# Orders of VectorE and ScalarE around seven waits of TensorE in a two-layer mixer and FFN kernel

## The reference, cut to what matters

```python
mod = (silu(c) @ ada_w[l] + ada_b[l])            # 6 vectors of 1024: shift, scale, gate, twice
h = rms_norm(x, mix_pre_g) * (1 + scale_m) + shift_m
q, k, v, x_lru, gate = split(h @ w_in)
attn = sliding_window_attention(rope(q), rope(k), v, sinks)      # window 128
lru  = rg_lru(causal_dwconv(x_lru)) * gelu(gate)                 # recurrence over the tokens
y = concat(rms_norm(attn), rms_norm(lru)) @ w_out
x = x + gate_m * rms_norm(y, mix_post_g)
h = rms_norm(x, ffn_pre_g) * (1 + scale_f) + shift_f
g, val = split(causal_dwconv(h @ w_up))                          # 2 x 3072
x = x + gate_f * rms_norm((gelu(g) * val) @ w_down, ffn_post_g)
```

## Time and profile before

| | |
|---|---|
| median of 3 runs | 1156.53 us |
| profiled execution, its own time | 1151.1 us |
| its span | 1149.3 us |
| TensorE (PE) busy | 1115.9 us, 97% |
| VectorE (DVE) busy | 803.3 us, 70% |
| ScalarE (ACT) busy | 569.6 us, 50% |
| `lo_chunk`, L1146 | 221.0 us, 182 of 1221 ns |
| `split_step`, L604 | 189.6 us, 182 of 1053 ns |
| mean granted clock of TensorE | 0.991 of full speed |

### The profile page before, as it was taken

One profiled execution on the slowest core, in us unless ns is written; L12 is line 12 of the kernel. 1 busy time (PEld: TensorE's weight loads), 2 busy tenths in 40 slices (PEclk: granted clock), 3 DMA queues, 4 the chain that ended last, 5 costly groups with the idle time before them and its releaser, 6 DMA issues.

```text
span 1149.3 us, 14253 instructions
## 1 busy us (share of the span) xinstructions
PE 1115.9 (97%) x5638; PEld 936.3 (81%) x5638; DVE 803.3 (70%) x1229; ACT 569.6 (50%) x958; POOL 52.1 (5%) x110
## 2 busy tenths in 40 slices
PE   6999899999999999999998999999999999999997
PEld 6986688888788888888888777898888888888886
DVE  7999987777678776777565797777643665356545
ACT  4488948544134422343377895765422444134431
POOL 3000110000210011000000000000000000000000
PEclk7999999999999999999999999999999999999999
DMA  9853373333765558643132421322232232233221
GB/s 357 337 205 110 100 285 111 128 112 127 270 242 202 167 191 290 158 150 125 55 111 74 93 74 59 102 98 92 96 106 92 92 103 81 91 114 107 92 92 74
DMA packets 49284, 159.88 MB, mean 139 GB/s; under 512 B 9409, under 2 KB 9665, under 8 KB 49217
## 3 DMA queue, kind: packets, MB, share of 16 engines
q1 hardware_dynamic: 33968, 118.57, 30.7%
q0 software_dynamic: 10368, 37.75, 9.9%
q10 hardware_dynamic: 4880, 2.64, 0.9%
HBM read 156.83 MB, written 2.11 MB: 138 GB/s over the span
## 4 chain that ended last, share of the span: by engine, by line
PE 77%; DVE 13%; ACT 5%; DMA 4%; issue 2%; SPq 0%; DVEq 0%; ACTq 0%
PE ps L1832 48%; PE ps L1857 27%; DVE sb_wL L1146 3%; DMA sb_raw<-in_w 1%; ACT sb_wH L604 1%; DMA sb_vw<-in_ada 1%; DMA sb_adaw<-in_ada 1%; DVE sb_x L1224 1%; DVE sb_stage L1152 1%; DVE sb_adaw L1152 1%; PE ps L1945 1%; DVE sb_y L1191 1%; ACT sb_sq L736 1%; DVE sb_xc L1452 1%; DVE sb_vw L1152 0%
## 5 line engine op out<-in xcount | busy, mean ns | idle before, releaser
L1832 PE MATMUL ps<-sb_hH,sb_wH 128*128 128x512 f32 x832 | 325.4, 391 | 0.5 <-ACT sb_xc L807 0.5
L1832 PE MATMUL ps<-sb_hL,sb_wH 128*128 128x512 f32 x832 | 323.8, 389 | 0.0
L1832 PE MATMUL ps<-sb_hH,sb_wL 128*128 128x512 f32 x832 | 323.8, 389 | 0.0
L1146 DVE TENSOR_TENSOR sb_wL<-sb_raw,sb_wH 128x1024 fp32r<-128x1024 f32 x182 | 221.0, 1221 | 78.7 <-ACT sb_wH L604 78.3
L604 ACT ACTIVATE sb_wH<-sb_raw 128x1024 fp32r<-128x1024 f32 x182 | 189.6, 1053 | 163.5 <-DMA sb_raw<-in_w 163.3
L1857 PE MATMUL ps<-sb_wH,sb_mH 128*128 128x512 f32 x512 | 202.2, 395 | 4.6 <-DVE sb_wL L1146 4.6
L1857 PE MATMUL ps<-sb_wL,sb_mH 128*128 128x512 f32 x512 | 199.4, 389 | 0.0
L1857 PE MATMUL ps<-sb_wH,sb_mL 128*128 128x512 f32 x512 | 199.4, 389 | 0.0
L1832 PEld LDWEIGHTS ps<-sb_hH,sb_wH 128*128 128x128 f32 x832 | 156.2, 188 | 37.6 <-issue 4.3
L1832 PEld LDWEIGHTS ps<-sb_hH,sb_wL 128*128 128x128 f32 x832 | 156.2, 188 | 32.5
L1832 PEld LDWEIGHTS ps<-sb_hL,sb_wH 128*128 128x128 f32 x832 | 156.2, 188 | 31.8
(11 more groups left out here) (222 smaller groups left out, 1136.5 us busy)
## 6 DMA issues: line engine op xcount, KB each, us to landing
sb_raw<-in_w SPq DMA_DIRECT2D x182, 512.0 KB, 3.5
sb_adaw<-in_ada POOLq DMA_DIRECT2D x42, 512.0 KB, 4.9
sb_stage<-in_ada SPq DMA_DIRECT2D x24, 512.0 KB, 14.2
sb_vw<-in_ada POOLq DMA_DIRECT2D x20, 512.0 KB, 4.9
sb_raw<-in_w SPq DMA_DIRECT2D x8, 384.0 KB, 14.3
sb_stage<-in_ada POOLq DMA_DIRECT2D x6, 512.0 KB, 4.2
sb_x<-in_x SPq DMA_DIRECT2D x4, 512.0 KB, 5.6
sb_x<-in_xt SPq DMA_DIRECT2D x4, 512.0 KB, 6.6
```

Of the source, the lines that this page charges most:

```text
L1146: TT(low_of(n), raw_of(n), high_of(n).bitcast(fp32), ALU.subtract).then_inc(w_lo, 1)
L1832: return nc.tensor.matmul(out, a, b, start=start, stop=stop, **kw)
```

## The change

The same instructions are issued as before; on ScalarE and VectorE some stand elsewhere. TensorE, SyncE and POOL keep their programs.

```diff
 # ScalarE, tile_chains, k = 1 (once: the end of the first layer)
                     y_square(l, k, 1, 2)
                     y_root(l, k, 2)
+                    split_step(n0 + 4)
                     x_root(l, k, 2)
                     x_scaled(l, k, 2)
+                    split_step(n0 + 5)
                     y_square(l, k, 1, 3)
                     y_root(l, k, 3)
+                    tmp_lower(l, k, 2)
...
                 x_root(l, k, 3)
                 x_scaled(l, k, 3)
-                if k:
-                    split_step(n0 + 4)
-                    split_step(n0 + 5)
-                tmp_lower(l, k, 2)
+                if not k:
+                    tmp_lower(l, k, 2)
 # ScalarE, mixer of the first layer
                     copy_pt(1)
                     gate_tanhs(1)
-                    decays(1)
                     square_out(1)
                     attn_high(1)
                     gate_tanhs(2)
+                    decays(1)
+                    gate_out(1)
                     split_step(O0 + 3)
                     decays(2)
-                    gate_out(1)
                     gate_out(2)
 # VectorE, tile_chains
                 x_update(l, k, 3)
-                x_recip(l, k, 3)
                 if k:
                     lo_chunk(n0 + 4)
+                x_recip(l, k, 3)
+                tmp_upper(l, k, 2)
+                if k:
                     lo_chunk(n0 + 5)
-                tmp_upper(l, k, 2)
 # VectorE, mixer of the first layer
                     mod_unit(25)
-                    drives(1)
+                    attn_low(1)
                     gated(1)
                     mod_unit(26)
-                    attn_low(1)
                     gated(2)
+                    drives(1)
...
                     drive(0)
+                    attn_low(2)
                     scan(0)
                     drive(1)
-                    attn_low(2)
...
                     product(1)
+                    lo_chunk(O0 + 5)
                     product(2)
-                    lo_chunk(O0 + 5)
 # VectorE, mixer of the second layer
                     scan(3)
+                    lo_chunk(O0 + 5)
                     lru_fold(2)
                     product(3)
-                    lo_chunk(O0 + 5)
 # VectorE, behind the mixer, both layers (late() has work in the first alone)
                 lo_chunk(O0 + 6)
+                lo_chunk(O0 + 7)
                 late(11, 1)
-                lo_chunk(O0 + 7)
 # VectorE, first two down projections of a layer (units() has work in the first layer alone)
                         fh, pair = divmod(r, 2)
+                        for c in ahead[r]:
+                            lo_chunk(B + down_no(g, 0) + c)
                         units(down_no(g, 2 * r))
                         units(down_no(g, 2 * r + 1))
-                        for c in ahead[r]:
-                            lo_chunk(B + down_no(g, 0) + c)
```

## The result

The changed kernel takes 1143.72 us in the median of 4 runs (1141.80 to 1144.63), the kernel before 1156.34 (4 runs, 1156.04 to 1157.63): the ratio is 0.9887 [0.9869, 0.9904]. In a second session it was 0.9908 [0.9890, 0.9927], 1143.63 against 1155.15 us. So 11.5 to 12.6 us are gained. One execution of the kernel before, at 1871.6 us and a mean clock of 0.556, is left out of every ratio and count.

The account below looks back on a forecast made before the run. TensorE, busy 97% of the span, was taken as the bound, so only its waits could be won: -5.4 - 0.6 + 0.75 - 1.4 - 1.1 = -7.7 us, from 1156.53 to 1148.8 us; 8-in-10 range 1144.8 to 1152.6.

Parts of the forecast that it names:

- The distance of the profile to the median: Whole kernel: the median of the runs was taken to lie 5.4 us above the profiled execution, after the change too.
- End of the first layer, 5.4: Ahead of tile 3's transposes: 4.0 of TensorE's 4.10 us wait go, plus 1.4 us of low clock; 5.4 us won.
- Second mixer, 1.07: Second layer's mixer: an earlier low part removes TensorE's whole wait at 705.68; 1.07 us won.
- First mixer, 0.6: First layer's mixer: five waits aimed at, but ScalarE is nearly always busy, so only 0.6 us won.
- behind it -0.75: Behind the first layer's mixer: VectorE idles for chunk 7's split, so its later chain slips; 0.75 us lost.
- The wait of 0.61 for chunk 7: TensorE's wait at 164.20, behind the first layer's mixer: to shrink by 0.4 us, about half.
- the one at 193: TensorE's wait of 0.85 us at 193.32: to grow by about that much more, taking back what was won ahead.
- Down projections, 1.4: First layer's down projections: low parts ahead of ada products remove TensorE's wait of 1.43 us at 307.89; 1.4 us won.
- rival 2: Both down projections: evictions behind ada products make TensorE wait 2.0 and 1.6 us; 1152.4 us in all, chance 15%.
- hidden: After the down projections' passes: VectorE some 4 us late into the convolution taps, at no cost to TensorE.
- Rival 1: Whole kernel: every wait aimed at goes and nothing comes back; 12.7 us won, 1143.8 us, chance 7%.

Follow-up runs that it names:

- the part alone: For the end of the first layer: the kernel before with only that stretch's new order on ScalarE and VectorE; 1145.39 us, ratio 0.9919.
- ScalarE's alone: The kernel before with only ScalarE's reordering at the end of the first layer, VectorE's low parts in their old places; 1152.14 us, ratio 0.9978.
- the first mixer alone: The kernel before with only the first layer's mixer reordered, chunk 7's low part still behind the ada unit; 1153.69 us, ratio 0.9992.
- the second profile: The kernel before, unchanged, run and profiled again; its profiled execution took 1154.85 us, its median 1155.14 us, ratio 0.9998.

## Why the prediction was wrong

- **The distance of the profile to the median.** This is the step that failed: "the median of the runs lies 5.4 above it, so 1156.53 - 7.7 = 1148.8". It is not a constant of the kernel. It is in the main the low stretch of 4.8 us behind the wait at 705.68, which by their clocks some 53 of 74 executions have and the profiled one hadn't; the change removes it. What else is in the 5.4 stays open. Had I read the clean profile as what it was, 1151.1 less 7.7, the answer would have been 1143.4; measured 1143.7. That would have been partly luck: the profile lay 0.9 us above its own kind (1150.2), and 7.7 was 1.2 too much against it (1150.2 - 1143.7 = 6.5).
- **End of the first layer, 5.4.** Right in the profile: 5.75 between the two I compared, 5.7 with the part alone, by the mechanism and in both of its halves (2.0 of wait and 1.4 of clock for ScalarE's alone).
- **Second mixer, 1.07.** The wait went, as worked out. Mis-sized: alone it is worth 5.5 us (3.1 to 8.1), since it carried the low stretch. I had priced the clock behind the wait of 4.10 us, where the profile showed it, and not behind this one, where it didn't.
- **First mixer, 0.6, and behind it -0.75.** Not to be told from nothing. The part alone gives 0.9 (-0.6 to 2.5), the first half's stretch is 0.3 us longer in the mean, forecast 0.15. The mechanism is in the trace: `copy_pt(3)` starts at 138.30, right behind `gelus`, and the waits of 1.1 at the gates and of 0.4 for `mL` are replaced by 0.9 for `exps(3)`. A new wait for `copy_pt(3)` stands in the five profiles of the new order in which the clock is full there; in the changed kernel's two the low clock covers it. With the first mixer alone it is

```profile
139.26 1.09 PE L1832 MATMUL ps<-sb_adaw,sb_vw 128*64 128x256 f32 x8 [0.94 <-ACT sb_adaw L870]
```

  where before had 139.75. ScalarE is as full as in the earlier trace rows, 27.45 us:

```profile
110.24:138.20 27.96, 25.60 (x151) 19.31 (x152) 26.32 (x47) 27.45 (x52) 1.58 (x3) 0.96 0.37 122
```

  The loss behind the mixer is there in kind: from the end of chunk 7's split to the transposes it is 31.6 to 31.8 us in the five profiles with its new order and 30.6 to 31.4, mean 31.0, in the nine with the old, some 0.6 us where I had 0.76. The wait of 0.61 for chunk 7 is not halved but gone, and the one at 193 is 1.2 instead of 0.85 where no chunk is very late, about as forecast. What I had taken as fixed is the landing of chunk 6: TensorE's wait for it is 0.8 to 1.7 us in the three profiles with the diff's whole first half.
- **Down projections, 1.4.** The wait is gone in all seven profiles with the new order, and TensorE nowhere waits for an eviction, so rival 2 is refuted. But over seven profiles of the old order the two waits are 0.6 us and not 1.6: 7.2 us for that transfer was a slow landing, 5.7 in the second profile. And "hidden" was wrong for the convolution taps: in four of the seven new ones TensorE waits 0.3 to 1.2 us around 476 us for a tap of VectorE's (`sb_R`, L1776), a mean of 0.5. What is left is 0.1.
- **Rival 1** named 1143.8 us and is refuted all the same: the waits that it counts as gone came back at `exps(3)`, `copy_pt(3)` and chunk 6, and its number is met by the clock, which it doesn't name.

With the sizes measured: -5.7 - 1.1 - 4.8 + 0.3 - 0.1 = -11.4 us against an execution with the low stretch, where -11.5 and -12.6 were measured.

## What to carry to other kernels

If the profiled execution lies some way off the median of the timed ones, find out what the usual execution has in addition before adding the distance to a forecast; the mean clock beside each execution shows it (0.985 against 0.991 here), and a second profile shows where. A wait of 1 us of TensorE can cost more than four times its length in clock, in a part of the executions. Here it stood behind products of a single column; whether that matters, no run varied. And a transfer's landing in one profile is a draw: terms that hang on it need several profiles.

## What was not expected

- Behind a wait of 1.08 us TensorE ran at 1.2 GHz for some 10 us in 4 of 7 profiles, at a cost of 4.8 us; behind the wait of 4.10 us at the layer's end the clock had cost 1.4 us, less than a third of that.
- The executions of one instruction order, parted by their mean clock, have medians 5.3 us apart (1155.5 and 1150.2).
- The same chunk of 512 KB landed 6.1 to 8.5 us after its issue in eleven profiles with three ada units ahead of it, and at most 5.6 in a twelfth; the next one landed 3.5 us after its own with the units behind it.
